# Linear attention in seven-slice heads: where the steps of a head stand among the projection slices

## What is computed

```python
def gla_chunked(q, k, v, log_a, strict):          # C = 64 tokens a chunk
    b = jnp.cumsum(log_a.reshape(B, H, n, C, dk), axis=3)
    q_e = q * jnp.exp(b)
    k_e = k * jnp.exp(-b)
    A = jnp.einsum('bhnid,bhnjd->bhnij', q_e, k_e) * tri
    o_intra = jnp.einsum('bhnij,bhnjv->bhniv', A, v)
    U = jnp.einsum('bhnjd,bhnjv->bhndv', k * jnp.exp(b_last - b), v)
    # scan over the chunks: S <- decay * S + U, keeping S before each chunk
    o_inter = jnp.einsum('bhnid,bhndv->bhniv', q_e, S_prev)
    return (o_intra + o_inter).reshape(B, H, T, dv)

o_g = rmsnorm(o_f + o_b, gla_out_norm) * silu(gg)  # forward and backward scans summed
return jnp.concatenate([o_attn, o_gla], axis=-1) @ w_out
```

## Time and profile before

| what | value |
|---|---|
| time, median of 3 runs | 2272.56 us (2271.38 to 2273.05) |
| the profiled execution | 2270.66 us, of which 2268.8 us is the span of the trace |
| mean granted TensorE clock | 0.989 of full speed |
| busy, share of the span | PE 98%, DVE 62%, ACT 36%, POOL 14% |
| chain of work that ended last | PE 88%, DVE 7%, issue 2%, ACT 2%, DMA 1% |
| idle time of PE ahead of L2498 | 3.7 us, once, ended by DVE's carries L2046 |
| idle time of PE ahead of L2179 | 2.5 us in three pieces, ended by DVE's adds L1621 |

### The profile page before, as it was taken

One profiled execution on the slowest core, in us unless ns is written; L12 is line 12 of the kernel. 1 busy time (PEld: TensorE's weight loads), 2 busy tenths in 40 slices (PEclk: granted clock), 3 DMA queues, 4 the chain that ended last, 5 costly groups with the idle time before them and its releaser, 6 DMA issues.

```text
span 2268.8 us, 35141 instructions
## 1 busy us (share of the span) xinstructions
PE 2217.8 (98%) x13468; PEld 2006.1 (88%) x13468; DVE 1411.2 (62%) x2366; ACT 810.7 (36%) x1566; POOL 310.6 (14%) x296
## 2 busy tenths in 40 slices
PE   5999999999999999999999999899999999999998
PEld 4999999999888878877778888899999999988887
DVE  7655565565575778766646755755555555557576
ACT  6222222223333446644433222532222222233343
POOL 5100011000100002100011113411121111110000
PEclk8999999999999999999999989999999999999999
DMA  3322322322785656522345843122322322377554
GB/s 122 97 79 79 103 87 88 109 84 79 264 266 177 195 155 175 186 70 80 116 136 175 283 128 128 65 79 78 103 85 90 108 85 79 97 277 263 170 189 164
DMA packets 247033, 305.65 MB, mean 135 GB/s; under 512 B 24274, under 2 KB 159954, under 8 KB 246868
## 3 DMA queue, kind: packets, MB, share of 16 engines
q1 hardware_dynamic: 238228, 290.29, 40.1%
q10 hardware_dynamic: 8640, 13.11, 1.6%
HBM read 208.97 MB, written 91.10 MB: 132 GB/s over the span
## 4 chain that ended last, share of the span: by engine, by line
PE 88%; DVE 7%; issue 2%; ACT 2%; DMA 1%; SPq 0%; POOL 0%; DVEq 0%; POOLq 0%; ACTq 0%
PE ps L2229 15%; PE ps L2230 15%; PE ps L2228 15%; PE ps L2238 7%; PE ps L2240 7%; PE ps L2239 7%; PE ps L2161 4%; PE ps L2163 3%; PE ps L2162 3%; PE ps L2427 1%; PE ps L2399 1%; PE ps L2407 1%; PE ps L2179 1%; PE ps L2181 1%; PE ps L2180 1%
## 5 line engine op out<-in xcount | busy, mean ns | idle before, releaser
L2228 PE MATMUL ps<-hs,w_hi 128*128 128x384 f32 (+1 forms) x1232 | 380.0, 308 | 2.8 <-DVE hs L1648 1.9
L2229 PE MATMUL ps<-hs,w_hi 128*128 128x384 f32 (+1 forms) x1232 | 379.7, 308 | 0.0
L2230 PE MATMUL ps<-hs,w_lo 128*128 128x384 f32 (+1 forms) x992 | 305.8, 308 | 0.0
L2238 PE MATMUL ps<-w_hi,dh 128*128 128x512 f32 x770 | 300.7, 391 | 2.0 <-DVE w_lo L1781 0.8
L2240 PE MATMUL ps<-w_hi,dh 128*128 128x512 f32 x770 | 299.7, 389 | 0.0
L1679 DVE TENSOR_TENSOR w_lo<-w_raw,w_hi 128x512 fp32r<-128x512 f32 x178 | 135.1, 759 | 176.8 <-ACT w_hi L1209 174.4
L2239 PE MATMUL ps<-w_lo,dh 128*128 128x512 f32 x610 | 237.4, 389 | 0.0
L1209 ACT CAST w_hi<-w_raw 128x512 fp32r<-128x512 f32 x220 | 135.7, 617 | 282.4 <-PE ps L2230 278.1
L2228 PEld LDWEIGHTS ps<-hs,w_hi 128*128 128x128 f32 x1232 | 232.6, 189 | 3.7 <-issue 3.7
L2229 PEld LDWEIGHTS ps<-hs,w_hi 128*128 128x128 f32 x1232 | 232.8, 189 | 0.0
L1778 DVE TENSOR_TENSOR dh<-dr,dh 128x640 fp32r<-128x640 f32 x154 | 126.9, 824 | 166.8 <-ACT dh L1240 166.7
(11 more groups left out here) (263 smaller groups left out, 4604.1 us busy)
## 6 DMA issues: line engine op xcount, KB each, us to landing
dr<-hid_mid SPq DMA_DIRECT2D x154, 320.0 KB, 3.2
w_raw<-in_w_ffn_down SPq DMA_DIRECT2D x176, 256.0 KB, 3.5
hid_mid<-st SPq DMA_DIRECT2D x88, 320.0 KB, 2.2
w_raw<-in_w_ffn_gate SPq DMA_DIRECT2D x44, 512.0 KB, 4.8
w_raw<-in_w_ffn_up SPq DMA_DIRECT2D x44, 512.0 KB, 5.2
hid_mid<-sg SPq DMA_DIRECT2D x66, 320.0 KB, 2.2
hq<-o_mid SPq DMA_DIRECT2D x70, 128.0 KB, 3.2
w_raw<-in_w_in SPq DMA_DIRECT2D x14, 512.0 KB, 4.4
```

Of the source, the lines that this page charges most:

```text
L2228: mm(out, hi[:, k, :], b_hi, start=k == 0 and j in (GP1, GP6, GP5), stop=False, skip_group_check=True)
L2229: mm(out, hi[:, k, :], b_lo, start=False, stop=False, skip_group_check=True)
L2230: last = mm(out, lo[:, k, :], b_hi, start=False, stop=k == 3, skip_group_check=True)
L2238: mm(out, hi, w_h, start=first and p in D_FRESH, stop=False, skip_group_check=True)
```

## The change

A head gets seven slices in place of eight (`H_SLICES`), so that heads 0, 1, 2 and 3 begin at slices 7, 14, 21 and 28 in place of 8, 16, 24 and 32. Its outputs go to `k` = 6, together with the third piece of the next head's scores; `keep_lo` and both spills go to `k` = 5, ahead of `load_k_in`. The last head's carries are cut over six steps in place of four, its outputs stand at `k` = 7, its norm at `k` = 9, and its spread and scaling from `k` = 10; there are 41 steps. The output projection uses its two pairs of banks in turn from slice 31 on, in place of 35. No product, no vector operation and no transfer is added or left out. The line numbers of the changed kernel are higher by one.

```diff
--- before.py
+++ after.py
@@ -81,7 +81,8 @@
 U_END = U_FFN2 + 4 * GROUPS
 PAIRS = HEADS // 2
 UNITS = PAIRS * TT
-GSTEPS = 43
+H_SLICES = 7
+GSTEPS = 41
 
 
 
@@ -411,7 +412,7 @@
         def D_BANK(w, c):
             return (3, 1, 4)[c] if w == 0 else D + (NCH * w + c) % 2
 
-        TWO_PAIRS = P2_SLICES + 9
+        TWO_PAIRS = P2_SLICES + 5
 
         def slice_bank(i):
 
@@ -558,8 +559,8 @@
         fw, bw = slice(0, DK), slice(DK, P)
 
         def gla_place(i):
-            h = min(i // 8 - 1, GLA_HEADS - 1)
-            return h, i - 8 * (h + 1)
+            h = min(i // H_SLICES - 1, GLA_HEADS - 1)
+            return h, i - H_SLICES * (h + 1)
 
         steps = []
         for n in range(1, max(SEQ_CHUNKS)):
@@ -567,7 +568,7 @@
                 if n < b - a:
                     steps += [("fw", a + n), ("bw", b - n)]
         CARRY = (0, 7, 13, 20, 26, len(steps))
-        CARRY_LAST = (0, 8, 16, 24, len(steps))
+        CARRY_LAST = (0, 6, 12, 17, 22, 27, len(steps))
 
         def carried(h, k):
 
@@ -910,12 +911,12 @@
                     load_gk(h + 2)
                 if k == 5 and h + 2 < GLA_HEADS:
                     load_k_out(h + 2)
-                if k == 6 and h >= 1:
+                if k == 5 and h >= 1:
                     spill_hi(h - 1)
+                if k == 5 and h >= 1:
+                    spill_lo(h - 1)
                 if k == 6 and h + 2 < GLA_HEADS:
                     load_k_in(h + 2)
-                if k == 6 and h >= 1:
-                    spill_lo(h - 1)
 
             for i in range(P2_SLICES - 3):
                 gla_loads(i)
@@ -1097,7 +1098,7 @@
                     gate(h - 1)
                 if k == 2 and h >= 1:
                     gla_root(h - 1)
-                if k == 7 and h == GLA_HEADS - 1:
+                if k == 9 and h == GLA_HEADS - 1:
                     gate(h)
                     gla_root(h)
 
@@ -1522,7 +1523,7 @@
                     chunk_decays(h + 1)
                 if k == 5 and h >= 1:
                     keep_hi(h - 1)
-                if h >= 0 and k == (5 if h == GLA_HEADS - 1 else 7):
+                if h >= 0 and k == (7 if h == GLA_HEADS - 1 else 6):
                     keep_o(h)
 
             for i in range(P2_SLICES):
@@ -2084,9 +2085,9 @@
                     carry(h, k)
                 if k == 2 and 0 <= h < GLA_HEADS - 1:
                     query(h + 1)
-                if k >= 8:
-                    scaled(h, k - 8)
-                if k == 6 and h >= 1:
+                if k >= 10:
+                    scaled(h, k - 10)
+                if k == 5 and h >= 1:
                     keep_lo(h - 1)
 
             for n in range(UNITS - 8, UNITS):
@@ -2540,9 +2541,9 @@
                         scores(h + 1, k - 4)
                 if 2 <= k <= 4 and h >= 1:
                     spread(h - 1, k - 2)
-                if k >= 8:
-                    spread(h, k - 8)
-                if h >= 0 and k == (5 if h == GLA_HEADS - 1 else 7):
+                if k >= 10:
+                    spread(h, k - 10)
+                if h >= 0 and k == (7 if h == GLA_HEADS - 1 else 6):
                     outputs(h)
 
             pe.wait_ge(const_set, ONES)
```

## The result

The changed kernel takes 2279.0 us in the median of 7 runs (2276.79 to 2283.73), the kernel before beside it 2272.4 us (7 runs): a ratio of 1.0029, with a 95% interval of 1.002 to 1.0038. It is 6.6 us slower; 2281 had been forecast. The profiled execution has a span of 2275.0 us against 2268.8, which is 6.2 us more.

What follows compares the result with a forecast made beforehand. PE was taken as the bound, busy 98% of the span, so only waits and clock could change: waits +7.0 us and one clock drop of 3.1 make +10.1 on 2270.66, rounded to 2281 us; range 2270 to 2289.

Steps and rivals of the forecast that it cites:

- The sign: The changed kernel would measure slower than the kernel before, above 2277.1 us; chance 0.65.
- the mechanism of the waits: A carry issued on DVE while POOL subtracts a weight tile waits until POOL is done; each meeting costs about 2 us.
- Head 0: PE waits 0.9 us for head 1's query and 1.2 us ahead of head 0's outputs: 2.1 us, as little as 0.
- Head 1: PE waits 2.5 us ahead of head 1's outputs for carries held by POOL's subtraction of slice 20; ends 0.2 and 3.3.
- The keys of head 3: Load issued later, scaling beside POOL's gate: the sums of squares of head 1 wait 1.5 us, or 0 without the meeting.
- Head 2: Carries beside slice 25's subtraction: waits of 1.9, 1.4 and 0.8 us, 4.1 against 2.5 before, so +1.6 us.
- Last head: PE waits 3.0 us in place of 3.7 ahead of the last outputs: -0.7 us, ends -3.7 and +0.5; half clock stays.
- The clock: One more drop to half clock, 2.5 us into head 1's outputs, costing 3.1 us; a short one 1.7, two up to 10.
- The banks: Output projection's banks in turn from slice 31 gain nothing, as no row after 1310 has PE waiting for an add.
- Rival (b): The 3.7 us wait ahead of the last outputs and the half clock behind it go: 8.7 us less, 2262 alone; chance 0.12.

Runs made afterwards that it cites:

- e1: Changed kernel with one weight tile's cut (ACT's rounding, POOL's subtraction) moved from slice 20 to 22: 2278.0 us, ratio 1.0029 to the kernel before.
- e4: Changed kernel with the last head's carries cut 14, 6, 4, 4, 4 over five steps in place of six: 2270.8 us, ratio 0.9997 to the kernel before.
- e2: Changed kernel with SP's load of head 3's keys ahead of the low part's write again: 2278.9 us, ratio 1.0033 to the kernel before.
- e3: Changed kernel with the weight tile's cut of slice 25 moved to slice 28: 2276.8 us, ratio 1.0026 to the kernel before.
- e6: Changed kernel with the output projection's banks in turn from slice 35 again, not 31: 2272.8 us, ratio 1.0004 to the kernel before.
- e8: Kernel before (eight slices a head), last head alone changed: carries 10, 7, 5, 5, 5, outputs at step 7, work moved along: 2259.1 us, ratio 0.9946.
- e10: e8 with the carries of heads 0 to 2 cut 14, 4, 4, 5, 5: 2260.3 us, ratio 0.9948 to the kernel before.
- e9: e8 with the last head's carries cut 6, 6, 5, 5, 5, 5 and `keep_lo` at step 6: 2265.0 us, ratio 0.9973 to the kernel before.

## Why the prediction was right, and where its terms were off

The sign, the range and the mechanism of the waits held: each wait that was worked out is there, ended by the instruction that was named. That the median came within 2 us of the 2281 is in part luck: of the 10.1 us worked out for the profiled execution 6.2 came, and the clock's share of them at another place than the one named. Term by term, expected and measured in the changed kernel's profile:

- *Head 0*, 2.1 us: 0.31 ahead of the scores and 0.90 ahead of the outputs, 1.2. The place was right; DVE's chain ran 0.4 us earlier (1197.43 in place of 1197.84).
- *Head 1*, 2.5 us: 2.19, and e1 shows the cause by taking it away. The high end of 3.3 does not follow from the rows: one subtraction of 2.46 us, wherever it falls among the carries, gives 2.5.
- *The keys of head 3*, 1.5 us out of 0 to 1.6: 2.34. The term was sized too low; by its own numbers (1270.7 + 2.91 + 1.49 is 1275.1 and not 1275.6) it was 1.1. The gate began 0.15 us before the first scaling (1266.03 and 1266.18), so that the first and not the second was held, and the second and the copies came behind it. The other order is hardly cheaper: in e4, where the first scaling began first and the second was held, the wait is 2.19, since the first scaling held the gate as well (4.16 us in place of 2.91), which the working left out. The gate counts like the subtraction, with 4.10 us against 1.49 for the scaling. The Trainium skill ("Advanced Engine Details and Errata", GPSIMD Details) says that Pool conflicts with DVE instructions that have two SBUF inputs; the trace agrees, with these 4.10 us. e2 shows that SP's order set it up.
- *Head 2*, 1.6 us over the 2.5 of before: 1.72 + 1.09 + 0.43 = 3.24, so 0.7 more. The carries beside the subtraction took 4.63 us as told; the three waits were 0.2 to 0.4 us shorter than worked out.
- *Last head*, -0.7: 2.78 in place of 3.7, so -0.9.
- *The clock*, 3.1 us inside head 1's outputs: not in this execution, where they run at 1.00. A new drop of 3.4 us stands behind head 2's sums of squares, 1.7 us, without a wait ahead of it. That the drop can come where it was forecast is seen in e2, at the same wait; in e3, e4 and e6, which have that wait too, the outputs ran at full clock. So it came in one profiled execution of five.
- *The banks*, "gain nothing": this step failed. They were judged by whether PE waited for adds before, and not by where the lateness of DVE goes when PE no longer waits for adds. e6 shows that they cost about 6 us, since the whole wait then stands in one piece ahead of the outputs.

The waits sum to +5.3 us where +7.0 had been worked out, the clock to 1.7 where 3.1 had.

Rival (b), the last wait going with the half clock behind it, was worth the 8.7 us named: e4 gives 8 us and e8, from the kernel before, 13. The change did not reach it because its six cuts put more adds between the carries; e4, with five cuts and the outputs at the same step, does.

## What to carry to other kernels

When a schedule by hand is made shorter, list for every step what each other engine does at that moment on its own calendar: a piece of POOL work that is tied to slice numbers falls on a different step when the steps move, and a DMA that stands behind a write in its queue moves with that write. A chain of many small operations that ends in front of a thin product (one of few columns), and for which that product waits, belongs as early as its engine is idle, not evenly over the steps (e4 and e8; in e10, where no outputs waited, it brought no gain that could be told). And where a wait cannot be removed, let it fall among dense products, in pieces, rather than in front of thin ones: here 1.9 us in three pieces in place of 2.8 in one were worth 6 us (e6). Whether the pieces did it or the shorter last wait was not parted: in e9, 1.4 us in one piece left the clock up in the outputs as well.

## What the runs showed of the hardware

Two operations that meet on DVE and POOL hold each other in either order. In the changed kernel the gate began first and the scaling of the keys waited; in e4 the scaling began first, and the gate itself is longer, 4.16 us in place of 2.91, and holds the second scaling, 4.20 in place of 1.48:

```profile
1269.26 4.16 POOL L1083 TENSOR_TENSOR go<-go,gg 128x1280 f32<-128x1280 f32 x1 [10.17 <-ACT gsq L1508]
1270.57 4.20 DVE L2016 TENSOR_TENSOR k_out<-gla_tmp,k_out 128x1280 f32<-128x1280 f32 x1
```

An add, which reads one input from PSUM, kept its duration: in the changed kernel one takes 0.69 us at 1313.59, beside a gate from 1313.29 to 1316.19, and the one before it, at 1312.28 with POOL idle, 0.69 too.

The granted clock falls at places that are not the same in every execution: outputs behind a wait of 2.19 us ran at 1.00 in the changed kernel and at 0.57 in e2. Over the 12 profiled executions the part from 1160 to 1400 us shows two kinds of drop. Drops of 3.4 us stand behind the sums of squares, 20 products of one column that take 2.4 us, and mostly without a wait of PE ahead of them: at 1279.8 in the kernel before, at 1321.5 in the changed one, at 1327.1 in e10. One alone stands elsewhere, at 1297.3 in e1, behind a wait of 1.7 us for an add. Longer ones, 6.8 to 13.7 us, stand only where PE had waited over 2 us ahead of the outputs or the sums: behind the waits of 2.8 to 3.7 us ahead of the last outputs in all five executions that have one (13.7 us each), behind the 2.19 us ahead of head 1's outputs in one of five (e2), and behind the 2.2 to 2.4 us ahead of head 1's sums of squares in two of five (10.2 in e1, 6.8 in e3). Behind the waits of 1.4 us and less ahead of outputs there is none. What decides it in one execution or another stays open.

The spread of the runs does not tell of such a wait by itself: 10.0 us in e9 and 8.4 in e2, which keep waits ahead of outputs, and 1.7 in e8, which has none, but 1.9 in e1, which keeps the 2.8 us ahead of the last outputs.
